# A hybrid decoder layer on one core: tiles of the second heads' k and v placed between the steps of the first attention, and late adaLN rows loaded in slices through SyncE's queue

## The reference, cut to what matters

```python
mod = silu(c) @ w_ada + b_ada                 # six rows of 1024: sh1, sc1, g1, sh2, sc2, g2
h = rmsnorm(x, norm1_g) * (1.0 + sc1) + sh1
q, k, v, ga, gb, z, xbc, dt = split(h @ w_in)
ya = diff_attention(q, k, v)                  # 8 heads; q and k: rmsnorm and rotary per head, two softmaxes per head
yb = ssd_mixer(z, silu(causal_conv(xbc)), dt) # 4 groups, 4 chunks of 128 tokens each
merged = sigmoid(ga) * (ya @ w_a) + sigmoid(gb) * (yb @ w_b)
x = x + g1 * (merged @ w_out)
h2 = rmsnorm(x, norm2_g) * (1.0 + sc2) + sh2
x = x + g2 * moe_ffn(h2)
```

## Time and profile before

| what | us |
|---|---|
| median of 3 runs | 1921.34 (1916.59 to 1923.87) |
| the profiled execution: its own time | 1925.31 |
| its span | 1923.5 |
| PE busy in it | 1599.4 (83%) |
| DVE busy | 1322.2 (69%) |
| ACT busy | 933.5 (49%) |
| mean granted TensorE clock | 0.918 of full speed |

### The profile page before, as it was taken

The page is one execution under the profiler, slowest core; times in us unless marked ns, Lnnn a source line. Parts: engine busy times, 40 slices in busy tenths (PEclk is TensorE's granted clock), DMA queues, the critical chain, the costliest instruction groups (busy, mean ns, idle before and its releaser), DMA issues.

```text
span 1923.5 us, 22704 instructions
## 1 busy us (share of the span) xinstructions
PE 1599.4 (83%) x7242; PEld 1250.0 (65%) x7243; DVE 1322.2 (69%) x1714; ACT 933.5 (49%) x1136; POOL 307.8 (16%) x298
## 2 busy tenths in 40 slices
PE   6888798699999999998974728999999779999950
PEld 1665586477777777775763527787777558877740
DVE  2675467677675766756456747788888438888849
ACT  2325434532334343342332127788888448888830
POOL 1000000011020201101100261222223122222210
PEclk9888899799999999997986859999999889999985
DMA  8211012069312121220421049899999549999848
GB/s 275 82 47 44 22 66 88 1 241 321 102 37 88 66 88 66 66 66 22 177 84 66 1 175 361 308 376 375 359 365 378 187 178 379 368 361 357 343 171 359
DMA packets 103538, 361.43 MB, mean 188 GB/s; under 512 B 19116, under 2 KB 29552, under 8 KB 76432
## 3 DMA queue, kind: packets, MB, share of 16 engines
q1 hardware_dynamic: 71472, 278.41, 39.0%
q0 software_dynamic: 27040, 62.07, 8.8%
q10 hardware_dynamic: 4928, 19.78, 2.6%
HBM read 352.18 MB, written 43.66 MB: 206 GB/s over the span
## 4 chain that ended last, share of the span: by engine, by line
PE 58%; DMA 17%; DVE 14%; ACT 4%; issue 4%; POOL 2%; SPq 0%; ACTq 0%; POOLq 0%; DVEq 0%
PE psum L1320 15%; PE psum L1322 15%; PE psum L1321 15%; DMA rawm<-in_w_exp_up 9%; DMA rawm<-in_w_exp_down 2%; DVE ring L886 2%; DMA modraw<-in_w_ada 2%; POOL slot_table L578 2%; PE psum L727 2%; PE psum L1353 2%; PE psum L1562 2%; DVE ofin L969 1%; PE psum L1507 1%; ACT ring L814 1%; PE psum L1495 1%
## 5 line engine op out<-in xcount | busy, mean ns | idle before, releaser
L886 DVE TENSOR_TENSOR ring<-rawm,ring 128x2048 fp32r<-128x2048 f32 x192 | 436.2, 2287 | 42.1 <-ACT ring L814 41.7
L814 ACT ACTIVATE ring<-rawm 128x2048 fp32r<-128x2048 f32 x192 | 368.0, 1918 | 96.5 <-DMA rawm<-in_w_exp_up 41.0
L1320 PE MATMUL psum<-ring,xT 128*128 128x512 f32 x528 | 223.7, 424 | 28.0 <-DVE ring L886 22.9
L1647 DVE TENSOR_TENSOR hl<-raw,hl 128x2048 fp32r<-128x2048 f32 x59 | 135.4, 2296 | 118.3 <-ACT hl L1111 117.8
L1322 PE MATMUL psum<-ring,xT 128*128 128x512 f32 x528 | 211.2, 400 | 0.0
L1321 PE MATMUL psum<-ring,xT 128*128 128x512 f32 x528 | 210.6, 399 | 0.0
L1320 PE MATMUL psum<-hl,hT 128*128 128x512 f32 x416 | 167.4, 402 | 20.7 <-DVE hT L1950 11.2
L673 POOL DMA_INDIRECT y_rows<-yb,row_of x64 | 99.3, 1551 | 438.4 <-ACT yb L858 429.5
L1322 PE MATMUL psum<-hl,hT 128*128 128x512 f32 x416 | 164.2, 395 | 0.0
L1321 PE MATMUL psum<-hl,hT 128*128 128x512 f32 x416 | 164.0, 394 | 0.0
L1320 PEld LDWEIGHTS psum<-ring,xT 128*128 128x128 f32 x528 | 102.1, 193 | 55.6 <-DVE ring L886 23.1
(11 more groups left out here) (374 smaller groups left out, 3093.4 us busy)
## 6 DMA issues: line engine op xcount, KB each, us to landing
rawm<-in_w_exp_gate SPq DMA_DIRECT2D x64, 1024.0 KB, 12.2
rawm<-in_w_exp_up SPq DMA_DIRECT2D x64, 1024.0 KB, 15.1
rawm<-in_w_exp_down SPq DMA_DIRECT2D x64, 1024.0 KB, 10.0
raw<-in_w_in SPq DMA_DIRECT2D x36, 1024.0 KB, 5.1
modraw<-in_w_ada POOLq DMA_DIRECT2D x16, 1024.0 KB, 7.0
ysum<-y_rows ACTq DMA_DIRECT2D x16, 1024.0 KB, 9.0
raw<-in_w_ada SPq DMA_DIRECT2D x8, 1024.0 KB, 9.6
raw<-in_w_branch_b SPq DMA_DIRECT2D x8, 1024.0 KB, 5.1
```

The costliest lines, as they stand in the source:

```text
L814: A(ring[:, slot, 1, :], rawm[slot][:], ACT.Copy).then_inc(S["m_hi2"], 1)
L886: TT(ring[:, slot, 0, :], rawm[slot][:], ring[:, slot, 1, :].bitcast(F32), ALU.subtract).then_inc(S["m_lo2"], 1)
L1320: M(dst, lhs(0), rhs(0), start=first, stop=False)
L1647: TT(hl[:, slot, 0, :], raw[slot][:], hl[:, slot, 1, :].bitcast(F32), ALU.subtract).then_inc(S["lo_done"], 1)
```

## The change

What it does:

- Scores use bank pair (4, 5) alone, so that banks 0 and 1 are free for dense tiles in an attention; PE's scores of item n now wait for the exponentials of item n-1 (before: n-2). `attn` is split into single steps, so that other steps can stand between them.
- q of hf = 1 is computed in front of attention 0 (in a buffer of its own). The four k and four v tiles of hf = 1 stand in attention 0, as 16 half tiles (12 matmuls) behind steps 1 to 16.
- In attention 1: the 8 tiles of branch a of hf = 0 behind steps 0 to 7, the xs tiles of group 0 as 8 half tiles behind steps 8 to 15, the two bc tiles behind steps 17 and 19.
- Norm and rotary of q and k are cut per tile: `qks` (square, sum) and `qkd` (rotary products) behind each tile, `qkr` (root) and `qkn` (scaling) behind the fourth. In attention they, and DVE's part of a split, come one attention step late.
- The factor -0.125 goes into q's rotary table; DVE's reduce takes the minimum, and its scaling operation is gone; two small operations of the softmax weights become one.
- Late rows: 64 slices of w_ada (128 channels by 512 columns, 256 KB), one DVE operation each, loaded through SP's queue between the weight units, two in flight. 16 of them stand between branch a and ga, the other 48 in the SSD groups: two behind each z tile, one behind most other tiles. The sum over partitions is now a tile of banks 0 and 1, evicted by ACT.

The core of the diff:

```diff
+    def attention(hf, fills):
+        pending = []
+        for n in range(STEPS):
+            item("attn", hf, n=n)
+            now = 1 if n < 4 * HALF else 2
+            for s in pending[:now]:
+                steps.append(dict(s, lag=True))
+            pending = pending[now:]
+            for b, o, ui in fills.get(n, ()):
+                out(b, o, ui=ui)
+                steps[-1]["lag"] = True
+                if ui != 0:
+                    pending += norm_of(b, o)
+        steps.extend(pending)
...
+    b = qkv("q", 1)
+    out(b, 0)
+    item("qkT", 0)
+    for o in range(4):
+        if o:
+            out(b, o)
+        steps.extend(norm_of(b, o))
+    parts = [(b, o, ui) for b in [qkv(n, 1) for n in "kv"] for o in range(4) for ui in range(2)]
+    attention(0, {n: parts[n - 1:n] for n in range(1, len(parts) + 1)})
+    item("qkT", 1)
+    a0 = [branch_a(0, b) for b in range(2)]
+    x, y = xs(0), bc(0)
+    fills = {n: [(a0[n // 4], n % 4, None)] for n in range(8)}
+    fills.update({8 + n: [(x, n // 2, n % 2)] for n in range(8)})
+    fills.update({17: [(y, 0, None)], 19: [(y, 1, None)]})
+    attention(1, fills)
...
         for o in range(4):
             out(z, o)
+            mods(2)
             conv(g, *((0,), (1, 2), (3,), ())[o])
...
+            def load_mod(n):
+                if n >= len(late_mods):
+                    return
+                if n >= 2:
+                    sp.wait_ge(S["mod_used"], late_mods[n - 2]["mod"])
+                sp.dma_start(modraw[:, n % 2], late_mods[n]["src"]).then_inc(S[f"mod_in{n % 2}"], 16)
...
-                            wait(pe, S["p_exp"], 2 * (item - 1))
+                        wait(pe, S["p_exp"], 2 * item)
...
-                                dst = psum[:, (4, 0)[n % 2] + m, :]
+                            dst = psum[:, 4 + m, :]
...
-                            L(V.tensor_reduce(sm[:, n % 8, 0:2], psum[:, b0:b0 + 2, 0:w_], AX, ALU.max))
-                            TS(sm[:, n % 8, 0:2], sm[:, n % 8, 0:2], -0.125, None, ALU.mult).then_inc(S["nmax"], 1)
+                        V.tensor_reduce(sm[:, n % 8, 0:2], psum[:, b0:b0 + 2, 0:w_], AX, ALU.min).then_inc(S["nmax"], 1)
```

More of the change, by code:

```diff
@@ L124, in whole, with mods, mod_rows @@
         out(b, *range(b["nout"]))
[L126 to L146, removed]
+    def mods(count):
+        for j, k in itertools.islice(late, count):
+            u = dict(late=len(late_mods), mod=9 + len(late_mods), tag=j, k=k,
+                     src=w["w_ada"][k * P:(k + 1) * P, j * 512:(j + 1) * 512])
+            late_mods.append(u)
+            item("modu", j, u=u)
+    def mod_rows(j):
+        b = dict(kind="modp", tag=("modp", j), u=[], nout=1, out0=outs[0], steps=[])
+        outs[0] += 1
+        rows_of.append(b)
+        out(b, 0)
     for j in range(4):
@@ L152, in plan_steps @@
     item("h", 0)
[L153 to L171, removed]
+    late = iter([(j, k) for j in range(4, 12) for k in range(KD)])
@@ new lines, in plan_steps @@
+    for n in "qkv":
+        b = qkv(n, 0)
+        for o in range(4):
+            out(b, o)
+            if n == "q" and o < 2:
+                steps[-1]["ahead"] = True
+            steps.extend(norm_of(b, o))
+            if (n, o) in DT_AT:
+                item("dt", DT_AT[n, o])
+    b = qkv("q", 1)
+    out(b, 0)
+    item("qkT", 0)
+    for o in range(4):
+        if o:
+            out(b, o)
+        steps.extend(norm_of(b, o))
+    parts = [(b, o, ui) for b in [qkv(n, 1) for n in "kv"] for o in range(4) for ui in range(2)]
@@ new lines, in plan_steps @@
+    attention(0, {n: parts[n - 1:n] for n in range(1, len(parts) + 1)})
[6 more added lines that the diff above has]
+    attention(1, fills)
+    item("late_in", 0)
+    for b in range(2):
+        x = branch_a(1, b)
+        for o in range(4):
+            out(x, o)
+            mods(1)
@@ L172, in plan_steps @@
+    conv = lambda g, *qs: [item("conv", g, q=q) for q in qs]
+    silu = lambda g, *qs: [item("silu", g, q=q) for q in qs]
     for b in range(2):
@@ L174, in plan_steps @@
         for o in range(4):
-            out_mod(x, o)
-    item("spill", 0)
[L178 to L191, removed]
+            out(x, o)
+            mods(1)
+            if b == 1 and o < 2:
+                conv(0, 4 + o)
+            elif b == 1:
+                silu(0, 2 + o)
+        if b == 0:
+            mod_rows(4)
+    item("spill", 0)
+    mod_rows(5)
     for g in range(G4):
@@ L379, in build @@
     modacc = sb("modacc", [P, 2, T])
-    modraw = nc.alloc_sbuf_tensor_at("modraw", [P, 2, UNIT], F32, offset=modraw_at)
-    sb.at = work
+    modraw = sb("modraw", [P, 2, T])
+    sb.at = xbc_at
     gb_sig = sb("gb_sig", [P, 4, T])
@@ L480, in build @@
         x2_at = USED - 2 * NT - NT
+        spill_at = sum(1 for s in itertools.takewhile(lambda s: s["kind"] != "spill", steps) if stages_out(s))
         def route(v, L):
@@ L1724, in _ @@
                     continue
-                if kind == "split":
+                if kind == "lo":
                     split_lo(s["u"])
```

395 lines of the change are left out of this document (216 added, 179 removed).

## The result

The changed kernel takes 1898.13 us (median of 4 runs, 1894.70 to 1903.58) against 1919.98 before (4 runs, 1916.59 to 1923.87): a ratio of 0.9888, 95% interval 0.9856 to 0.992. It is faster by 1.1%, inside the forecast range of 1862 to 1908, and 15 us above the forecast of 1883.

What follows compares the result with a forecast made beforehand. PE was taken as the bound up to the merge wherever it has dense tiles, the attentions as latency. Terms summed to -38.0, from the profiled 1925.3 to 1887.3; the median 4.0 lower gave 1883, range 1862 to 1908.

Steps and rivals of the forecast that it cites:

- (a): First q's norm cut per tile: PE's 9.0 us stall shrinks by 6.5 to 2.5 us, half a cold start counted; -7.9.
- (b): Attention 0 with the eight k and v tiles: 105.2 us instead of 109.3, bare start and DVE's lateness included; -4.1.
- (c): Attention 1 with branch, xs and bc tiles inside: 94.1 us instead of 119.4, PE being the bound; -25.3.
- (d): Branch a of hf = 0 no longer begins cold behind attention 0: -2.8; a possible cold start at qkT: +2.0.
- (e): Stretch from attention 1 to z's first matmul, late rows moved away: 70.0 us instead of 88.3; -18.3.
- The sums: Sums over partitions of late rows: 0.5 us each, the six that come later +2.8.
- (f): z tiles: six slices in front of the last silu put 4.7 us on PE's path in three groups; +14.1.
- (g): The other 24 slices, one behind a tile, where PE is not seen to wait for DVE: +1.5 (0 to +6).
- (h): SP's queue: 256 KB slices taken as landing in time, by an estimate of 2.6 us; no term in the sum.
- the first (serial chain): One pair of score banks makes attention steps serial: 0.6 us in each of 32 steps, +19, 1902; chance 0.18.
- the third (late slices): Slices landing at 7.0 us come late at z pairs (20 us) and branch a (6): 1909; chance 0.08.
- the fourth (the clock stays low): Fills don't lift the attentions' granted clock: 1925 at 0.8, 1954 at 0.7, deciding from 0.81 down; chance 0.08.

Runs made afterwards that it cites:

- The early q: Changed kernel with the second heads' four q tiles in front of the first heads' v instead of behind them: 1887.56 us, ratio 0.9827.
- the tiny other slices: Changed kernel with the 24 slices not behind z tiles in groups 0 to 2 worked on in one column of 512: 1879.11 us, not comparable as a total.
- spread slices: Changed kernel with the 48 slices in four groups of 12 instead of three of 16, none in front of the last convolution: 1887.09 us, ratio 0.9807.
- both combinations: Changed kernel with second heads' q before v and four groups of 12 slices: with single sums and parts 0, 1 emptied 1882.24 us; with row 8's sum later 1877.61.

## Why the prediction was right, and where it was off

The result is in the range and the likeliest case came true, with its mechanisms. The sum of -38.0 was too good: by 9 us against the two profiles, of which 4.6 is scatter behind the merge; by 14 up to the merge (1040.6 to 1016.4); and by 16 against the medians (-21.9).

- *(a)* -7.9, measured -10.0. The stall is 2.3 us for a forecast 2.5, PE goes on at the full clock behind it, and the section began 0.7 earlier. Counting half of the cold start was too cautious. The prediction says that no row tells what 2.5 us of idling do to the clock; the trace of before had such rows, and they show both outcomes (last section).
- *(b)* -4.1, measured -4.5, with its parts: the start is 11.1 us for 10.2 and begins cold; the waits for head rows are 10.0 in four, the run-out 4.0 of them for 5.5. Step 11's lateness, forecast at 3.2, is the two waits of 2.2 and 0.9: DVE has the root, the rows, a split and k's root in a row from 235.5 to 243.7 and only then takes item 12's minimum. The clock is low not only at the start but also behind the first head's wait (1.12 at 216.54 for what takes 0.66) and in the run-out. Attention 0 is 104.8 us for 105.2. The early q shows that the bare norm made 9.8 of the start's 11.1.
- *(c)* -25.3, measured -24.0: waits for head rows 7.2 in four. The first three are the forecast's 5.7; the last, 1.6, was to be covered by a bc tile and wasn't.
- *(d)* -2.8, measured -2.3. The +2.2 at the transposes of q and k agrees with the +2.0 by luck: the start at the lower clock behind attention 0 makes 1.2, and the rest is the first transposes, where PE waits 2.2 us (149.35) since ACT's high part (1.9 us) stands in front of their eviction. That wait was not foreseen.
- *(e)* 70.0 forecast, 72.4 measured. The 2.27 us wait for the last slice before row 5's sum wasn't in it.
- *The sums* are the term that was most mis-sized. I took 0.5 us for one and 2.8 for six. A sum takes 0.9 to 1.0 (445.81 to 446.77) and two in a row meet a full bank, 1.24 more: 3.3 in each of three groups, 9.9 where I had 2.8. Of the 7.1 between, 3.7 are the waits for the bank, which comes with the new sums' way through banks 0 and 1. The rest is a misreading of the old sum at 423.55, shown below.
- *(f)* +14.1, measured 3 x 3.8 for the waits and 2.4 + 0.9 + 0.9 for the starts at the lower clock: 15.6. The mechanism is as told, its two sizes were not: 3.8 of the six slices' 4.7 us show, and I had no term for the clock. The text's "1.2 at most in each group" holds for groups 0 to 2; the earlier trace rows ends at 820, and group 3's wait, given as 1 among the signs, was 3.1 before and stays 3.1.
- *(g)* +1.5, measured 3.4: a slice in part 1 makes PE wait 1.1 us for the staging copy, in each of three groups. Its removal removes the wait (the tiny other slices). With the sums and (f) that is 28.9 of the 29.9; the last 1.0 isn't traced.
- *(h)* held: 2.9 us to land, DVE waits 4.2 us for slices in all, 3.4 of them at the third slice. The Trainium skill, "DMA: Bandwidth & Descriptors", section "Anatomy of one DMA", gave an estimate of 2.6; the nearest row of the trace, 5.1, was farther off. The section states its figures for DMAs that GpSimd issues; issued by POOL, 256 KB took 3.2 and 1 MB 7.0, for its 2.6 and 4.4, so there the measurements decide. Slices below the 1 MB that the Trainium skill wants under the same title, "Rules for kernel authors", cost little here: DVE found all but two of the 64 in place.

The old sum again, with the rows behind it:

```profile
423.55 1.02 PE L1367 MATMUL psum<-modacc,ones 128*128 128x512 f32 x2
424.01 0.79 PE L1320 MATMUL psum<-hT,hl 128*128 128x512 f32 x1
424.64 0.40 PE L1321 MATMUL psum<-hT,hl 128*128 128x512 f32 x1
```

The tile's first matmul begins 0.5 us behind the sum, but takes 0.79 instead of 0.40. Its second begins 1.09 behind the sum, and within a tile matmuls follow each other every 0.23: the sum held PE for 0.86 us and not for 0.5. The start of the next row alone is no measure of a price where matmuls overlap.

The rivals: the first (serial chain) is real, 0.8 us a step when bare in the kernel before and 0.5 in the changed one, and hidden by tiles; the third (late slices) did not occur, and where POOL issued the slices they took little longer to land, it was POOL's own order that cost PE its time; the fourth (the clock stays low) did not: 0.90 and 0.98 in the attentions, above its border of 0.81.

What stays open is why a start behind a short wait is cold once and not the other time, and so some 5 us of any single comparison of two profiles.

## What to carry to other kernels

Latency-bound steps and dense tiles are worth interleaving even when the interleaving itself costs something (a bank pair here: when bare 26 us in the kernel before, 16 in the changed one), but price the seams: the last norm before the first step, and short tiles that stand alone between two long ones. Work moved to a "free" engine is free only behind the operation that the bound engine waits for, not in front of it: the same 48 slices, with their sums, cost 12.5 us more or less by their place. And give transfers that wait for a consumer a queue on an engine that has nothing else in order.

## What the hardware did that I had not expected

The start behind a wait of the same length is at either clock. In the changed kernel, behind the wait for z_rows in groups 0 and 1:

```profile
533.94 3.63 PE L1605 MATMUL psum<-ident,z_rows 128*128 128x128 f32 x16 [2.52 <-DVE z_rows L1981]
```

```profile
651.68 1.97 PE L1605 MATMUL psum<-ident,z_rows 128*128 128x128 f32 x16 [2.53 <-DVE z_rows L1981]
```

2.5 us of idling, 16 transposes in 3.63 or 1.97 us; the kernel before has both kinds too. The thirteen profiles together, groups 0 to 2:

| PE waited | for | goes on at the lower clock |
|---|---|---|
| 1.2 us | the silu (before, spread slices, both combinations) | 0 of 12 |
| 2.5 us | z_rows (all profiles) | 19 of 39 |
| 5.0 us (one 6.6) | the silu (the seven with six whole slices in front) | 21 of 21 |

In group 3 the same 2.5 us wait for z_rows is followed by the lower clock in all thirteen. A start at the lower clock there costs 1.6 us: the twelfth dense matmul begins 6.0 us behind the first transpose instead of 4.3. So gains of 1 to 2 us by a shortened wait may be moved to another place rather than won, as in three of the experiments, while bringing a wait from 5.0 to 1.2 gave its clock back each time.

A DVE operation that touches SBUF alone and begins while POOL works does not end before POOL's does. In the changed kernel, a slice's first operation, which takes 0.48 us at 579.41, stands in a part beside POOL's product:

```profile
491.79 2.12 DVE L1712 TENSOR_SCALAR modacc<-modraw,silc 128x512 f32<-128x512 f32 x1
```

```profile
491.55 2.07 POOL L1115 TENSOR_TENSOR ua<-upper,aa 128x1024 f32<-128x1024 f32 x1 [7.24 <-PE psum L1570]
```

It ends 0.3 us behind POOL's. The state's scaling has the same, in the kernel before too (2.39 at 540.08, for 0.68 at 549.93). An operation of DVE that reads PSUM isn't lengthened: 0.69 at 550.65 in the kernel before, which ends 1.1 us ahead of POOL's. The Trainium skill, "SBUF — State Buffer", section "SBUF: two separate sides", says that the port pair of the two is held by one instruction at a time and the other waits; these rows agree. No experiment here was made on it.
